# The last boundary of a two-block model: token tiles first in the MLP's end, dz between dk's halves

## The reference

```python
def sq_relu_mlp(h, w1, w2):
    return jnp.square(jax.nn.relu(h @ w1)) @ w2
...
x = x + rmsnorm(sq_relu_mlp(h, mlp_w1[l], mlp_w2[l]), g[3])          # end of the first model
...
h = rms_norm(x, g_pre) * (1 + scale[:, None, :]) + shift[:, None, :] # start of the second
... = jnp.split(h @ w_in, cuts, axis=-1)      # q, k, v, z, beta, a of the delta rule, then the rest
qkv_dn = jax.nn.silu(causal_depthwise_conv(qkv_dn, conv_w))
g = (-jnp.exp(a_log) * jax.nn.softplus(a_logit + dt_bias)).transpose(0, 2, 1)
o_dn = gated_delta_rule_chunked(l2_normalize(q_dn), l2_normalize(k_dn), v_dn, g, beta)
```

## Time and profile before

| | us |
|---|---|
| median of 3 runs | 940.37 (939.91 to 942.44) |
| the profiled execution | 937.9 |
| its span, first to last instruction | 936.1 |
| TensorE busy | 898.9 (96%) |
| VectorE busy | 631.3 (67%) |
| ScalarE busy | 483.0 (52%) |
| mean granted clock of TensorE | 0.993 of full |

### The profile page before, as it was taken

The page is one execution under the profiler, slowest core; times in us unless marked ns, Lnnn a source line. Parts: engine busy times, 40 slices in busy tenths (PEclk is TensorE's granted clock), DMA queues, the critical chain, the costliest instruction groups (busy, mean ns, idle before and its releaser), DMA issues.

```text
span 936.1 us, 14545 instructions
## 1 busy us (share of the span) xinstructions
PE 898.9 (96%) x6258; PEld 800.5 (86%) x6258; DVE 631.3 (67%) x782; ACT 483.0 (52%) x629; POOL 32.2 (3%) x25
## 2 busy tenths in 40 slices
PE   5999999999999999999999999999789999989997
PEld 5989888799999998988789999999689998877775
DVE  4798746578666676696667767676669584546563
ACT  7665456473343334754557334344467863437441
POOL 0000000000000000000000000000000244000000
PEclk9999999999999999999999999999999999999999
DMA  9544543466666665454345666665434343334331
GB/s 376 187 175 136 181 135 135 140 243 225 225 225 225 230 224 178 161 176 156 114 180 192 241 231 241 244 234 196 153 113 162 109 151 126 131 102 146 112 114 45
DMA packets 23727, 165.47 MB, mean 177 GB/s; under 512 B 2640, under 2 KB 2896, under 8 KB 4336
## 3 DMA queue, kind: packets, MB, share of 16 engines
q1 hardware_dynamic: 22176, 159.39, 48.4%
q0 software_dynamic: 1056, 4.34, 1.3%
q10 hardware_dynamic: 432, 0.82, 0.2%
HBM read 163.49 MB, written 1.05 MB: 176 GB/s over the span
## 4 chain that ended last, share of the span: by engine, by line
PE 86%; DVE 7%; ACT 5%; DMA 1%; issue 1%; DVEq 0%; SPq 0%; ACTq 0%
PE lin L512 15%; PE lin L514 15%; PE lin L513 15%; PE acc L512 10%; PE acc L514 10%; PE acc L513 10%; DVE w_lo L1616 1%; PE acc L695 1%; ACT w_hi L1176 1%; DMA raw<-in_weights 1%; PE acc L754 1%; PE lin L627 1%; ACT arena L1563 1%; PE lin L597 1%; PE acc L1028 1%
## 5 line engine op out<-in xcount | busy, mean ns | idle before, releaser
L1616 DVE TENSOR_TENSOR w_lo<-raw,w_hi 128x2048 fp32r<-128x2048 f32 x138 | 318.6, 2317 | 155.1 <-ACT w_hi L1176 154.2
L1176 ACT CAST w_hi<-raw 128x2048 fp32r<-128x2048 f32 x138 | 262.6, 1906 | 178.1 <-DMA raw<-in_weights 106.9
L512 PE MATMUL lin<-h_hi,w_hi 128*128 128x256 f32 x736 | 210.4, 286 | 2.4 <-DVE h_lo L1662 1.9
L513 PE MATMUL lin<-h_lo,w_hi 128*128 128x256 f32 x736 | 208.6, 283 | 0.0
L514 PE MATMUL lin<-h_hi,w_lo 128*128 128x256 f32 x736 | 208.6, 283 | 0.0
L512 PEld LDWEIGHTS lin<-h_hi,w_hi 128*128 128x128 f32 x736 | 141.6, 192 | 3.4 <-DVE h_lo L1662 2.0
L513 PEld LDWEIGHTS lin<-h_lo,w_hi 128*128 128x128 f32 x736 | 141.6, 192 | 0.3
L514 PEld LDWEIGHTS lin<-h_hi,w_lo 128*128 128x128 f32 x736 | 141.4, 192 | 0.0
L512 PE MATMUL acc<-w_hi,f_hi 128*128 128x512 f32 x288 | 112.4, 390 | 0.0
L513 PE MATMUL acc<-w_lo,f_hi 128*128 128x512 f32 x288 | 112.2, 390 | 0.0
L514 PE MATMUL acc<-w_hi,f_lo 128*128 128x512 f32 x288 | 112.1, 389 | 0.0
(11 more groups left out here) (330 smaller groups left out, 1064.0 us busy)
## 6 DMA issues: line engine op xcount, KB each, us to landing
raw<-in_weights SPq DMA_DIRECT2D x150, 1024.0 KB, 4.8
rowbuf<-in_rows POOLq DMA_DIRECT2D x6, 512.0 KB, 4.4
x<-in_x_in SPq DMA_DIRECT2D x2, 512.0 KB, 4.6
arena<-in_const_even POOLq DMA_DIRECT2D x1, 1024.0 KB, 10.2
out<-x SPq DMA_DIRECT2D x2, 512.0 KB, 2.6
cst<-in_const ACTq DMA_DIRECT2D x1, 576.0 KB, 9.4
colbuf<-in_cols ACTq DMA_DIRECT2D x1, 159.0 KB, 5.9
msk<-in_masks POOLq DMA_DIRECT2D x1, 144.0 KB, 5.9
```

The lines of the kernel that those rows point to most:

```text
L512: pe.matmul(dst, st_hi, mv_hi, start=first, stop=False)
L513: pe.matmul(dst, st_hi, mv_lo, start=False, stop=False)
L1176: act.copy(w_hi[:, o % SPLIT, :], raw[:, j % RAW, :]).then_inc(hi_done, 1)
L1616: dve.tensor_tensor(w_lo[:, j % RAW, :], r, hi.bitcast(F32), ALU.subtract).then_inc(tile_split, 1)
```

## The change

- **Products by token tile.** `last_down` takes all four tiles down1_6 and down1_7 for token tile 0 and then for token tile 1. Both tiles of down1_6 are used up only in the second round. The transposes of token tile 0 stand before the last column half.
- **Lead.** `last_lead` takes dk for token tile 0, dz's first tile for token tile 0, the transposes of token tile 1, dz's second tile for token tile 0, dk for token tile 1, dz for token tile 1 with `lead_turned` between, and then the gates. dz stands before dq in the order of tiles and pairs.
- **h.** ScalarE writes scale and shift into the arena in float32; VectorE casts 512 columns to `h_hi` and takes one difference of 512 columns for `h_lo`.
- **POOL** computes `w_lo` of dk's first tile; VectorE only counts it.
- **Orders.** ScalarE and VectorE place their casts and splits one by one in the boundary. Behind it the convolution of dk stands before the gates on VectorE, the decay's transposes inside dq's second tile, the squares of q inside dv's second tile, and the copies of dk, dz, dq and dv have no `ahead` in front of them.

```diff
@@ plan_tiles, plan_lin: the order of the weight tiles and of the PSUM pairs
     feature_major("dk", "w_in", 512)
+    token_major("dz", "w_in", 1536)
     feature_major("dq", "w_in", 0)
-    token_major("dz", "w_in", 1536)
...
-    g += ["n2a0", "n2a1", "*dk", "dq", "dz", "dv", "*drow", ...
+    g += ["n2a0", "n2a1", "dz", "*dk", "dq", "dv", "*drow", ...
@@ POOL
                 elif i > 0:
+                    if i == 4:
+                        n = FIRST["dk"]
+                        hi = w_hi[:, ORDINAL[n] % SPLIT, :].bitcast(F32)
+                        pool.wait_ge(hi_done, ORDINAL[n] + 1)
+                        pool.tensor_tensor(w_lo[:, n % RAW, :], raw[:, n % RAW, :], hi, ALU.subtract).then_inc(pool_split, 1)
@@ TensorE: the end of the MLP and the lead
+            def last_down():
...
+                for t in range(TT):
+                    for j in range(2):
+                        for k in range(2):
+                            for c in range(2):
+                                mm = products(6, j, t, c, k)
+                        if t == 1:
+                            mm.then_inc(tile_used, 1)
+                    if t == 0:
+                        after(f_ready)
+                    for c in range(2):
+                        if t == 1 and c == 1:
+                            for b in range(2):
+                                turned(0, b, ("n2a0", "n2a1"), 3, True)
+                        for j in range(2):
+                            for k in range(2):
+                                mm = products(7, j, t, c, k)
+                            if t == 1 and c == 1:
+                                mm.then_inc(tile_used, 1)
+                        if t == 0 or c == 0:
+                            mm.then_inc(acc_done, 1)
+
+            def last_lead():
...
+                pe.wait_ge(pool_split, 1)
+                products(0, 0)
+                products(1, 0).then_inc(lead_done, 1)
+                project_token_major("dz", (0,), (0,))
+                for b in range(2):
+                    turned(1, b, ("n2a0", "n2a1"), 3, True)
+                project_token_major("dz", (1,), (0,))
+                products(0, 1).then_inc(tile_used, 1)
+                products(1, 1).then_inc(tile_used, 1)
+                project_token_major("dz", (0,), (1,))
+                lead_turned("dk")
+                project_token_major("dz", (1,), (1,))
...
-            lead("dk", ("n2a0", "n2a1"), 3, True)
+            last_lead()
             gates()
-            lead_turned("dk")
             fill("dq", 0)
-            fill("dq", 1)
             sum_squares("sqk")
-            after(sp_ready)
-            turned_columns(GATE_ACC["row"], gate("sum")).then_inc(crow_done, 1)
-            fill("dz", 0)
+            project_feature_major("dq", (1,), decay_turned)
             after(rows_ready)
             inverse_lengths()
-            fill("dz", 1)
             fill("dv", 0)
             after(erow_ready)
             to_columns((7, 8, 4, 3), S_AT["rows"], 512)
-            after(cols_read)
-            sum_squares("sqq")
-            after(cols_read)
+            after(cols_read, 2)
             columns_as_rows("drow", ...)
-            fill("dv", 1)
+            project_feature_major("dv", (1,), lambda: sum_squares("sqq"))
@@ ScalarE, boundary with a bias
-                        ins = act.activation(h_hi[:, k, t * P:(t + 1) * P], pair(names[t])[:, k * P:(k + 1) * P], ...
+                            ins = act.activation(arena[:, at:at + P], src, ACT.Identity, scale=gain(k), bias=bias(k))
...
+                    split_until(past(name, 1))
                     x_squares(0)
+                    x_root(0)
+                    split_until(past(name, 2))
                     sum_squares(name, 1, 0)
-                    x_root(0)
                     h_part(0, 0)
+                    h_part(0, 1)
                     sum_squares(name, 1, 1)
-                    h_part(0, 1)
                     tile_root(1)
+                    split_until(past(name, 3))
                     x_squares(1)
                     x_root(1)
+                    split_until(past(name, 4))
                     h_part(1, 0)
                     h_part(1, 1)
-                    split_until(past(name, 3))
@@ VectorE, boundary with a bias
-                            ins = dve.tensor_scalar(tmp(k), src(k), gain(k), bias(k), ALU.mult, ALU.add)
...
+                    link(dve.tensor_copy(hi, whole))
+                    dve.tensor_tensor(lo, whole, hi.bitcast(F32), ALU.subtract).then_inc(ht_ready, 1)
@@ ScalarE, behind the boundary
...
             root_lengths()
-            split_until(LAST["dz"] + 4)
-            copy_out("dv", at("pre", 1024, 2048))
+            copy_out("dv", at("pre", 1024, 2048), splits=False)
+            split_until(LAST["dv"] + 2)
             read_out(act, "dv")
@@ VectorE, behind the boundary
-            ahead("dk")
+            split_until(LAST["dz"] + 1)
+            conv("dk", S_AT["pre"], S_AT["k"], "convd", 4)
             after(gates_done)
...
-            split_until(LAST["dz"] + 4)
+            split_until(LAST["dv"] + 1)
             normalised("q", 128 ** -0.5)
             ahead("dv")
             filled(dve, "dkt")
```

More of the change, by code:

```diff
@@ L514, in passes, with project_feature_major @@
                 return pe.matmul(dst, st_lo, mv_hi, start=False, stop=last)
-            def project_feature_major(name, halves=(0, 1)):
+            def project_feature_major(name, halves=(0, 1), between=None):
                 if 0 in halves:
@@ L526, in project_feature_major @@
                             mm = passes(pair(name)[:, at:at + T], hi[:, c:c + P], lo[:, c:c + P], *chunk(k), k == 0, k == DC - 1)
+                        if between and b == 0:
+                            between()
                     mm.then_inc(tile_used, 1)
@@ L628, in turned, with lead_products, lead @@
                 mm.then_inc(xt_done, 1)
-            def lead(name, names, done, scaled=False):
-                def products(i, t, ks):
[L633 to L656, removed]
+            def lead_products(name, i, t, ks, ready):
+                hi, lo = split_tile(FIRST[name] + i)
+                at = t * 512 + i * 256
+                for k in ks:
+                    if i == 0 and k % 4 == 0:
+                        ready(k)
+                    w = slice(k * 256, (k + 1) * 256)
+                    st = [part[:, k, t * P:(t + 1) * P] for part in (h_hi, h_lo)]
+                    mm = passes(acc[:, at:at + 256], *st, hi[:, w], lo[:, w], k == 0, k == DC - 1)
+                return mm
+            def lead(name, names, done):
+                def products(i, t, ks):
+                    return lead_products(name, i, t, ks, lambda k: after(ht_ready) if k == 0 else read_out(pe, names[t]))
+                products(0, 0, range(8))
+                turned(1, 0, names, done)
+                products(1, 0, range(4))
+                turned(1, 1, names, done)
                 products(1, 0, range(4, 8)).then_inc(lead_done, 1)
@@ L659, in lead, with products @@
                 products(1, 1, range(8)).then_inc(tile_used, 1)
+            def last_down():
+                split = {}
+                def products(i, j, t, c, k):
+                    n = FIRST[f"down1_{i}"] + j
+                    if n not in split:
+                        split[n] = split_tile(n)
+                    h = [part[:, i % 2, 2 * j + k, t * P:(t + 1) * P] for part in (f_hi, f_lo)]
+                    w = slice(k * 1024 + c * 512, k * 1024 + (c + 1) * 512)
+                    at = t * 1024 + c * 512
+                    return passes(acc[:, at:at + 512], *h, split[n][0][:, w], split[n][1][:, w], False, i == 7 and j == 1 and k == 1)
+                for t in range(TT):
[18 more added lines that the diff above has]
+                            mm.then_inc(acc_done, 1)
@@ new lines, in last_lead, with products @@
+            def last_lead():
+                def products(i, t):
+                    return lead_products("dk", i, t, range(8), lambda k: after(ht_ready))
+                pe.wait_ge(pool_split, 1)
[10 more added lines that the diff above has]
+                project_token_major("dz", (1,), (1,))
@@ L1353, in swap_halves, with copy_out @@
                 act.copy(to[64:128, :], pair(name)[0:64, :]).then_inc(swap_ready, 1)
-            def copy_out(name, dst, func=ACT.Copy):
-                ahead(name)
+            def copy_out(name, dst, func=ACT.Copy, splits=True):
+                if splits:
+                    ahead(name)
                 filled(act, name)
@@ L2147, in _ @@
             magnitude()
[L2148 removed]
+            split_until(LAST["dz"] + 2)
+            split_until(LAST["dq"] + 1)
             rest_of_log1p()
```

86 lines of the change are left out of this document (48 added, 38 removed).

## The result

The changed kernel takes 945.98 us as the median of 5 runs (944.31 to 946.66); the kernel before took 941.6 beside it (939.91 to 943.48, 5 runs). The ratio is 1.0046, interval 1.0027 to 1.0065: slower by 4.4 us, under half a per cent, but clear of the noise. The forecast was 944.7 (940 to 949), a shift of +4.3. The profiled execution of after took 946.5, its span is 944.7, its mean granted clock 0.986 (0.993 before).

The account below looks back on a forecast made before the run. TensorE, busy 96% of the span, was taken as the bound: its products plus idle and low-clock time. Terms -7.9 + 0.2 + 2.1 + 8.5 = +2.9, plus 1.4 of clock, gave +4.3: 944.7 us, range 940.0 to 949.0.

Parts of the forecast that it names:

- Boundary, -7.9: End of the second MLP into dk and dz: TensorE's loss falls from 11.3 to 3.4 us, a gain of 7.9.
- I take the first and cost it at nothing: POOL's difference for dk's first tile: the faster form, 4.0 us, ending at 666.1, before dk wants it; cost 0 (0 to 3.4).
- Gates' log, +0.2: Between the gates and dv: the gates' log is ready at 710.4, leaving TensorE idle 0.2 us (0 to 1.5).
- drow, +2.1: Drow transposes, before dv ends: TensorE waits 2.1 us (1.5 to 3) for VectorE's copy.
- Before V, clock: Up to V, the end of dv: no low-clock term counted; V forecast at 730.8 against 736.4, 5.6 us earlier.
- Behind dv, +8.5: From the end of dv to Y's transposes: two new waits behind late ScalarE casts, together 8.5 us.
- First wait: Before the k k and k q products behind dv: TensorE idle 3.6 us for the normalised q.
- The second: Before the deg transposes behind dv: TensorE idle 4.9 us, VectorE reading dkt behind bk's first split, until V+21.0.
- 1.4 of clock: Behind dv: a clock lowering after the second wait costs 1.4 us, within bounds 0 and 3.2.
- More clock and port: Rival, chance 0.18: lowering after the second wait behind dv costs 3.2, not 1.4, POOL a microsecond: +6.9, 947.3.
- The clock decides the other way: Rival, chance 0.20: the change removes a longer lowering at the boundary, worth another 3.0, new idle causes none: 940.3, not slower.
- ScalarE's order does not bite: Rival, chance 0.07: behind dv, bq and bk are cast before they are wanted, so 8.5 falls away: 934.8.

Follow-up runs that it names:

- the first experiment: Changed kernel with ScalarE's casts of bq's two tiles put back before the q lengths' root and bk's first before the copy of dv: 936.11 us, 0.9963 of before.

## Why the prediction was right, step by step

- **Boundary, -7.9:** measured -8.1. The idle time before dk was put at 2.0, all of it for h_lo, and is 1.84 for x and 0.25 for h_lo. The first part has a cause that the sum left out: "I take the first and cost it at nothing" was wrong of POOL. Its difference took 4.59 us (4.0 was taken from the earlier trace rows) and ended at 669.0, 667.1 on the prediction's scale, where it wrote 666.1. What it did to VectorE was mis-sized: x's scale lost 2.5 us, not "up to a microsecond". The lock fits, sharing doesn't. Yet dk started at 671.8 on the prediction's scale (673.70 less 1.87), 0.6 behind the forecast 671.2 and not the 1.0 that the prediction gave for a lock. In the kernel's time POOL's help and its price cancel (the run without POOL), which is why the sum stayed right. dz's second split was put at 1.1 us idle and is 0.43: on the prediction's scale TensorE came 0.5 later (681.4, not 680.9) and the split ended 0.2 earlier (681.8, not 682.0).
- **Gates' log, +0.2:** there is no wait. **drow, +2.1:** the wait is 1.59.
- **Before V, clock:** the steps had none. Two lowerings of 3.4 us (703.2 and 727.1) cost up to 1.7 each, the half of their length. V came 3.2 us earlier by the same measure (86.68 us from 648.39 instead of 89.87), against 5.6 forecast. This is the step that was short. In the profiles of the ten kernels with the new boundary a lowering begins between 701.6 and 705.4 in seven and is missing in three, so it isn't a fixed property of the order.
- **Behind dv, +8.5:** measured 8.4 (28.3 less 19.95). First wait 3.38 against 3.6. The second was put at 4.9 and is 1.76, since the clock fell at the k k products, which took 2.9 longer. The prediction said so in words ("A lowering after the first is eaten by the second wait") but counted 4.9 and added 1.4 of clock on top. The end of the wait was right all the same: ScalarE's and VectorE's queues set it, and it came at V+20.7, where V+21.0 was written. The run with bq's casts ahead shows the 4.9 as 4.72 once the first wait is gone.
- **Sum:** up to Y +5.2 in the profile, corrected by the 1.87 at its start; +4.3 forecast. The median moved by +4.4. It came out by errors of both signs, in part by luck: V 2.4 us later than forecast, against the 1.4 of clock that was added a second time. By the means of all runs the change costs 1.8 us of product and 2.8 of rest; the steps taken together give +6.1 (the boundary without its 3.2 of clock, -4.7, then 0.2, 2.1, 8.5) and -1.8 (1.4 less 3.2). The size was right, its make-up was not: less in the product, and more time at the lower clock.
- **The rivals:** "More clock and port" fell in its mechanism: no lowering stands behind the second wait (1.00 from 755.80 to 763.40), and POOL costs the kernel nothing. Its own terms add up to +7.1 (2.9 + 3.2 + 1.0), not +6.9. "The clock decides the other way" fell: the rest grew. "ScalarE's order does not bite" fell with the first experiment, which also shows its price: 936.1 against the 934.8 written down for it.

## What to carry to other kernels

Moving work into a stall pays only if the engines that feed the next stretch keep their order: look at what each in-order queue has ahead of the first instruction that the next product needs, before the change and after, and put a cast for later ahead of a copy that waits, not behind it. Two waits in a row don't have to add (here 6.2 and 6.4 alone, 8.4 together): price each alone and both together. Idle time beside which the clock falls can cost more than itself (2.5 us of idle and 6 to 7.5 of time without the token order), so split every result into span x clock and the rest before explaining it.

## What the runs showed of the hardware

- POOL and VectorE on SBUF: a 128x1024 float32 scale took 3.27 us instead of 0.75, a 128x2048 difference 4.53 instead of 2.28, each next to a POOL difference of 4.59 to 4.60 us that wasn't slowed. In the kernel before POOL waits for VectorE in the same way (3.10 instead of 1.16). POOL is half as fast on the same work (4.59 against 2.28), and giving it a split that VectorE had to wait out gained nothing (934.76 with it, 933.55 without).
- The granted clock fell to half at 703.2, with TensorE busy in every record since 694.0 (from 698.70 to 703.20 there are 4.50 us of products in 4.50 us). So a fall isn't always preceded by idle time that the profile shows. What stands before it are the gates: products of 16 and 8 columns from 698.74 to 702.2. In the kernel before, such products stand at 384.4 to 388, and a lowering begins at 388.0; but the same products at 693.2 to 696.7 are followed by none. What decides it isn't shown.
- Stretches that are the same in two kernels can differ between profiles by a lowering (3.4 us at 423.3 and at 914.8, worth 1.6 us each). In the three series of 19 to 29 runs of the kernel before, the spans have a standard deviation of 1.6 to 2.1 us, their products with the clock 1.0 to 1.3.
